# Half of the top-k searches moved from VectorE to ScalarE, and the distance bias from TensorE to VectorE

## The reference

```python
dots = jax.nn.relu(jnp.einsum('bqhd,bsd->bqhs', qib, k_idx).astype(jnp.float32))
score = jnp.einsum('bqh,bqhs->bqs', wb.astype(jnp.float32), dots)
score = jnp.where(visible[None], score, -jnp.inf)
_, idx = lax.top_k(score, topk)
...
logits = jnp.einsum('bqhd,bqkd->bhqk', qb, kg).astype(jnp.float32) * (HEAD_DIM ** -0.5)
logits = logits - slopes[None, :, None, None] * dist[:, None]
probs = jax.nn.softmax(logits, axis=-1).astype(v.dtype)
```

## Time and profile before

| | us |
|---|---|
| median of 3 runs (lowest to highest) | 3513.35 (3512.68 to 3517.88) |
| the profiled execution | 3499.91 |
| its span | 3498.0 |
| PE, DVE, ACT, POOL busy | 3099.7, 2084.9, 1290.0, 123.4 |

### The profile page before, as it was taken

One profiled execution on the slowest core, in us unless ns is written; L12 is line 12 of the kernel. 1 busy time (PEld: TensorE's weight loads), 2 busy tenths in 40 slices (PEclk: granted clock), 3 DMA queues, 4 the chain that ended last, 5 costly groups with the idle time before them and its releaser, 6 DMA issues. The chain is left out here.

```text
span 3498.0 us, 44638 instructions
## 1 busy us (share of the span) xinstructions
PE 3099.7 (89%) x15457; PEld 2525.6 (72%) x15457; DVE 2084.9 (60%) x4217; ACT 1290.0 (37%) x2575; POOL 123.4 (4%) x245
## 2 busy tenths in 40 slices
PE   6798888888888887876889699999999999999997
PEld 3576676677666666665778588788878888788876
DVE  2168888889999998989545444324442444244422
ACT  1364445444454444453443222222222322232222
POOL 0000000000000000000001100000000000000000
PEclk8788889887888888797999899999999999999999
DMA  5011100000000000000046533334333433343333
GB/s 202 21 46 31 37 25 25 19 25 25 22 10 19 22 19 10 10 4 7 4 160 180 165 93 96 90 120 144 96 96 114 138 97 97 112 144 96 96 92 107
DMA packets 316083, 254.97 MB, mean 73 GB/s; under 512 B 9153, under 2 KB 271905, under 8 KB 315809
## 3 DMA queue, kind: packets, MB, share of 16 engines
q1 hardware_dynamic: 282544, 236.29, 21.9%
q10 hardware_dynamic: 33392, 16.81, 1.7%
HBM read 219.50 MB, written 33.57 MB: 72 GB/s over the span
## 5 line engine op out<-in xcount | busy, mean ns | idle before, releaser
L1125 DVE TENSOR_SCALAR_CACHE_REDUCE above<-score,cand 128x384 bf16<-128x384 f32 (+13 forms) x448 | 661.9, 1478 | 9.0
L1865 DVE TENSOR_TENSOR p_lo<-raw,p_hi 128x1024 fp32r<-128x1024 f32 x264 | 323.4, 1225 | 422.6 <-ACT p_hi L1791 422.4
L1791 ACT ACTIVATE p_hi<-raw 128x1024 fp32r<-128x1024 f32 x264 | 279.3, 1058 | 690.9 <-PE dbank L1762 351.9
L984 ACT ACTIVATE probT<-tbank 128x512 f32<-128x512 f32 (+3 forms) x448 | 217.5, 488 | 506.3 <-PE tbank L713 503.8
L1175 DVE TENSOR_SCALAR_CACHE_REDUCE logit<-lbank 128x512 f32<-128x512 f32 (+3 forms) x448 | 246.7, 553 | 199.5 <-PE lbank L698 197.2
L729 PE MATMUL obank<-vb,probT 128*128 128x64 f32 x2176 | 303.4, 283 | 8.0 <-ACT probT L984 7.1
L591 PE MATMUL work<-w_in,h_T 128*128 128x512 f32 (+1 forms) x768 | 303.5, 545 | 0.7 <-ACT h_T L793 0.7
L729 PEld LDWEIGHTS obank<-vb,probT 128*128 128x128 f32 x2176 | 293.0, 206 | 13.9 <-ACT probT L984 13.4
L1743 PE MATMUL gbank<-x_hi,p_hi 128*128 128x512 f32 x704 | 275.1, 391 | 29.1 <-DVE p_lo L1865 29.1
L1760 PE MATMUL dbank<-p_hi,a_hi 128*128 128x512 f32 x704 | 277.1, 394 | 17.0 <-DVE a_lo L1893 14.1
L1761 PE MATMUL dbank<-p_lo,a_hi 128*128 128x512 f32 x704 | 276.2, 392 | 0.0
(11 more groups left out here) (202 smaller groups left out, 5231.7 us busy)
## 6 DMA issues: line engine op xcount, KB each, us to landing
raw<-in_w_gate_up SPq DMA_DIRECT2D x176, 512.0 KB, 3.8
raw<-in_w_down SPq DMA_DIRECT2D x88, 512.0 KB, 3.7
ada<-in_w_ada ACTq DMA_DIRECT2D x32, 512.0 KB, 3.9
wada<-in_w_ada SPq DMA_DIRECT2D x4, 2048.0 KB, 15.5
x_in<-in_x SPq DMA_DIRECT2D x16, 512.0 KB, 3.8
mixT<-oT SPq DMA_DIRECT2D x32, 256.0 KB, 2.4
mix<-mixT SPq DMA_DIRECT2D x16, 512.0 KB, 6.5
x_rows<-in_x SPq DMA_DIRECT2D x16, 512.0 KB, 4.6
```

Of the source, the lines that this page charges most:

```text
L1125: link(nc.vector.tensor_scalar(above[:, 0:L], score[:, 0:L], cand[:].bitcast(F32), None, ALU.is_ge, ALU.add, accum_out=count[:]), between, 1)
L1791: nc.scalar.activation(p_hi[:, s], raw[:, s], ACT.Copy).then_inc(panel_high, 1)
L1865: nc.vector.tensor_tensor(p_lo[:, s], raw[:, s], p_hi[:, s].bitcast(F32), ALU.subtract).then_inc(panel_ready, 1)
```

## The change

Six things change.

1. Blocks with an odd number (3, 5, ... 15) are searched by ACT. One ACTIVATE with the function Sign over the L scores (L1108 of the new program, `sum_signs`) gives by its accumulator the number of scores below less the number above. POOL moves the candidate `pick` with three small instructions (`move_pick`), of which two stand behind the sum. After 32 bits DVE makes one last count (`count_next`, "above") and the ties.
2. The search of a block is spread over two iterations, b-2 and b-1, in proportion to weights (`slot_weight`: 3.0 for an A head, 2.5 + 0.45 (b+1) for a B head). So in each iteration one even block is searched by DVE and one odd block by ACT. `score` gets two buffers. A heads, projections and norms run one block further ahead (block b+2 in iteration b).
3. The third product of a piece is gone. DVE adds the bias as it reads the piece: one `tensor_tensor_reduce` in place of the copy, with the minimum of the negated logits as its sum, chained from piece to piece, so that the reduction over pieces is gone too. Where the slope was applied on PE, `w_uq` and the first columns of `w_in` are now divided by the slopes at the start.
4. The exponential is written in place, over `logit`, which has three buffers now; `prob` is gone.
5. The wait for `bias_ready` stands on DVE, no longer on PE.
6. POOL fills 31 powers of two at the start; the modulation's last steps move a little.

```diff
+def search_slots(b):
+    slots = []
+    for it in (b - 2, b - 1):
+        if it + 2 < NB:
+            slots += [(it, "A", h) for h in range(HEADS)]
+        slots += [(it, "B", h) for h in range(HEADS)]
+    vector, scalar = {}, {}
+    if searched_by_scalar(b):
+        wts = [slot_weight(kind, it) for it, kind, h in slots[:-2]]
+        for slot, r in zip(slots, spread(wts, len(ON_SCALAR))):
+            scalar[slot] = [(b, ON_SCALAR[n]) for n in r]
+        vector[slots[-2]] = [(b, AFTER_SCALAR[0])]
+        vector[slots[-1]] = [(b, action) for action in AFTER_SCALAR[1:]]
...
+                    link(nc.gpsimd.tensor_tensor(pick_next[:], pick[:], toward_int[:, max(k - 1, 0):max(k - 1, 0) + 1],
+                                                 ALU.add))
+                    pool.wait_ge(signs_summed, 32 * nth + j + 1)
+                    link(nc.gpsimd.tensor_scalar(pick_back[:], less_more[:], float(L - 2 * TOPK), toward[:, k:k + 1],
+                                                 ALU.is_gt, ALU.mult))
+                    nc.gpsimd.tensor_tensor(pick[:], pick_next[:], pick_back[:], ALU.subtract).then_inc(pick_ready, 1)
...
-                    nc.tensor.matmul(out, q_lo[kind][:, h, :], keys, start=False, stop=False)
-                    mm = nc.tensor.matmul(out, slope_id[:, h, :], bias_of(kind, b, o, n)[:, at:at + width],
-                                          start=False, stop=True)
+                    mm = nc.tensor.matmul(out, q_lo[kind][:, h, :], keys, start=False, stop=True)
...
+            def sum_signs(b, action):
+                act.wait_ge(relu_used, relus[0])
+                act.wait_ge(pick_ready, 34 * nth + j + 1)
+                nc.scalar.activation(signs[:, 0:L], score[:, b % 2, 0:L], ACT.Sign, scale=-1.0,
+                                     bias=pick[:].bitcast(F32), accum_out=less_more[:]).then_inc(signs_summed, 1)
...
-                nc.vector.tensor_scalar(logit[:, i % 2, o:o + n], lbank[m % 2][:, 0:n], 1.0, None,
-                                        ALU.mult, ALU.max, accum_out=(mx_sink[:, h, 0:1] if kind == "A" else mx[:, i % 2, c:c + 1])
-                                        ).then_inc(piece_read, 1)
+                least = mx[:, i % 2, c - 1:c] if c else neg_sink[:, h:h + 1] if kind == "A" else -LOWEST
+                into = negmax[:, i % 4:i % 4 + 1] if c == pieces - 1 else mx[:, i % 2, c:c + 1]
+                nc.vector.tensor_tensor_reduce(logit[:, i % 3, o:o + n], lbank[m % 2][:, 0:n], bias_of(kind, b, o, n),
+                                               scale=-SLOPES[h], scalar=least, op0=ALU.add, op1=ALU.min,
+                                               accum_out=into).then_inc(piece_read, 1)
```

More of the change, by code:

```diff
@@ L180, with searched_by_scalar, slot_weight, spread @@
 SEARCH = [("bit", j) for j in range(32)] + [("ties", 0), ("ties", 1)]
[L183 to L194, removed]
+ON_SCALAR = [("bit", j) for j in range(32)]
+AFTER_SCALAR = [("above", 0), ("ties", 0), ("ties", 1)]
+def searched_by_scalar(b):
+    return b % 2 == 1
+def slot_weight(kind, b):
+    return 3.0 if kind == "A" else 2.5 + 0.45 * (b + 1)
+def spread(weights, n):
+    whole, at, out = sum(weights), 0.0, []
+    for wt in weights:
+        first = round(n * at / whole)
+        at += wt
+        out.append(range(first, round(n * at / whole)))
+    return out
+def search_slots(b):
[11 more added lines that the diff above has]
+        vector[slots[-1]] = [(b, action) for action in AFTER_SCALAR[1:]]
+    else:
+        wts = [0.0 if (it, kind, h) == (b - 2, "B", HEADS - 1) else slot_weight(kind, it) for it, kind, h in slots[:-1]]
+        for slot, r in zip(slots, spread(wts, len(SEARCH) - 1)):
+            vector[slot] = [(b, SEARCH[n]) for n in r]
+        vector[slots[-1]] = [(b, SEARCH[-1])]
+    return vector, scalar
 MOD_STEPS = 4 * D // P
@@ L226, in front_a, with modulate @@
               5: [("proj", b, 3)], 6: [("proj", b, 4)]}.get(h, []))
[L228 to L231, removed]
-    for b in range(NB):
[L233 to L239, removed]
+    def modulate():
+        nonlocal mods
+        if mods < MOD_STEPS:
+            add(("mod", mods))
+            mods += 1
@@ L240, in mixing_steps @@
+    for b in range(2):
+        for h in range(HEADS):
+            steps.append(("head", "A", b, h, (), ()))
+            front_a(b + 1, h)
+            if b and h in (1, 7):
+                modulate()
+        steps += [("queries", "A", b + 1), ("gains", b + 1), ("latent", b + 1), ("latent_up", b + 1),
+                  ("norm", b + 2)]
+    for b in range(NB):
+        nxt = b + 2 if b + 2 < NB else None
+        if nxt:
+            steps.append(("scores", nxt))
+        else:
             steps.append(("queries", "B", b))
@@ L251, in mixing_steps @@
         for h in range(HEADS):
[L252 to L258, removed]
+            at = (b, "B", h)
+            steps.append(("head", "B", b, h, tuple(vector.get(at, ())), tuple(scalar.get(at, ()))))
@@ L531, in _ @@
                 if s[0] == "mod_rows":
+                    fill_affine()
+                    continue
+                if s[0] == "scores" and searched_by_scalar(s[1]):
+                    start_pick(s[1])
+                if s[0] == "head":
+                    for b, action in s[5] + tuple(x for x in s[4] if x[1][0] == "above"):
+                        move_pick(b, action)
+                if s[0:4] == ("head", "B", NB - 1, 0):
                     modulate()
-                    continue
                 if s[0] not in ("norm", "gains"):
@@ L1179, in maximum @@
[L1179 to L1184 removed]
+                if c == 0 and i >= 3:
+                    dve.wait_ge(pt_full, plan.group0[i - 2])
```

246 lines of the change are left out of this document (160 added, 86 removed).

## The result

| | before | after |
|---|---|---|
| median of 4 runs each, in turns, us | 3513.01 (3509.27 to 3517.88) | 3547.27 (3543.42 to 3552.1) |
| profiled execution (span) | 3499.91 (3498.0) | 3546.74 (3545.0) |
| last piece ends at | 1756.4 | 1797.7 |

The account below looks back on a forecast made before the run. PE was taken to bound A heads and DVE B heads. Terms -49 (A), -1 (B), -13 (blocks 14 and 15) and +4 (start) made -59 from 3499.9: 3441, plus 13.4 for the median, 3455 us; range 3420 to 3490, chance 0.40.

Parts of the forecast that it names:

- The step that failed: B heads: a phase lasts 8% longer than its busiest engine (4 to 12% seen), giving 32.4, 48.7 and 73.9 us.
- 1 us less for them and block 13's: All B phases together: -13 us from the search's move and +12 from the ties' wait, so -1.
- A heads: A phases, bound by PE: third products gone, search bits fewer, last phase 28 for 48.0 us; together -49 us.
- My bound of 2: A heads: the third product's 16 pieces per eight heads cost about 2 us a phase at the granted clock.
- Blocks 13 to 15: End of the kernel: iteration 13's B heads 7 us less, blocks 14 and 15 139 for 152.3 us, -13.
- Start: Before the first projection: scaling multiplications added, those on the unit matrix gone; 0 to 5.5 us, taken +4.
- The ties' wait: Last head but one of B phases: even blocks' ties wait for ACT, 2 us in iterations 1, 3, ... 11: +12.
- Sums of signs stall the pipeline: Rival, chance 0.17: B heads with alternating one and two sums cost the longer engine each; 54 us in iteration 8, 3525.
- The slow new piece: Rival, chance 0.10: DVE's new bias-adding piece runs at the scan's pace, 119 us more of DVE, +90: 3545.
- Free overlap: Rival, chance 0.20: A and B heads mix, idle time beside A heads serving B heads; 156 us at most, half gives 3375.
- POOL held up by DVE: Rival, chance 0.08: POOL's candidate steps behind a DVE scan wait up to 4.4 us, ACT behind them; +39, 3494.
- A bit's 1.94 us: B heads: price of one search bit on DVE for 1280 scores: count, accumulator read and two small steps.

Follow-up runs that it names:

- the second run: Changed kernel with the ties of even blocks put back in the last head, behind the norm they wait for: 3542.24 us, 1.0093.
- short signs: ScalarE sums signs of the first 128 columns only: changed kernel 3423.05 us, 0.9753; changed kernel with 9.0, 30.0, the ties last and the roots first 3344.34 us, 0.9531.
- the mended split: Changed kernel with A heads counting 9.0 instead of 3.0, ties last: 3469.69 us; with the roots first 3440.77; with 30.0 for VectorE's steps too 3434.13.
- the vector-only kernel: Changed kernel with every block searched by VectorE in one iteration, none by ScalarE, the new weights kept: 3592.31 us, 1.0234.
- 9.0: Changed kernel with the spreading's weight of an A head 9.0 instead of 3.0, ties of even blocks in the last head: 3469.69 us, 0.9877.
- the experiment with the third matmul: Changed kernel with each piece's first product made twice, so TensorE has the bias matmuls' work back: 3605.18 us, 1.0276.
- The vector-only kernel with the old split: Changed kernel, all search on VectorE in one iteration, old table for blocks 2 to 14 (21 or 18 of 34 steps beside A heads): 3510.76 us, 0.9998.
- 30.0: Changed kernel with A heads weighing 30.0 for VectorE's steps and 9.0 for ScalarE's, ties last, roots first: 3434.13 us, 0.9786.
- the ties last: Edit of the changed kernel: ties of even blocks go back to the last head, behind the norm they wait for; alone 3542.24 us, 1.0093.
- the roots first: Edit of the changed kernel: POOL does the gains' two roots before the pick steps of head B h0; alone 3543.2 us, with 9.0 and ties last 3440.77.
- the kernel before with a late split: Kernel before with its table alone changed, 10 search steps beside A heads and 24 beside B heads instead of 21 or 18 and 13 or 16: 3631.15 us, 1.0345.

## Why the prediction was wrong

**The step that failed** is "A phase is longer than its busiest engine ... I take 8%". The busy times it was applied to were good: iteration 3, ACT 30.0 forecast and 28.7 measured; iteration 8, DVE 45.1 and 42.7, ACT 41.8 and 41.3. The factor was 1.21, 1.40 and, in iteration 12, 1.42, instead of 1.04 to 1.12. For iterations 3 and 8 that gave 34.8 and 59.8 us for my 32.4 and 48.7; the B heads of blocks 0 to 12 grew by 97 us, where I had 1 us less for them and block 13's (some 20 of the 97 stood in the score phases before, as the second run shows). I had read the factor off stretches with one engine at 89 to 96%, so that it stood for the small gaps of an engine that nearly always has work. In the levelled stretch PE, which both others feed, waits for each of them in turn. These are its waits in the B heads of iteration 8, before (841.9 to 895.4 us) and after (925.9 to 985.7):

```profile
PE lbank L696 <- DVE logit L1175: 8.8, 4, 3.7
PE obank L729 <- ACT probT L984: 0.5, 1, 0.5
...
PE lbank L795 <- DVE mx L1315: 8.7, 4, 5.2
PE obank L826 <- ACT probT L1084: 8.4, 2, 4.8
```

Busy and waiting, PE makes up the stretch in both: 43.9 + 9.3 of 53.5 us, 42.5 + 17.1 of 59.8. With three engines at 41 to 43 of 60 us, each in order, and DVE and ACT with search steps between their own, nothing is hidden whole. The short signs put a number on it: 0.57 and 0.43 us of time for each microsecond of ACT's, with no engine over 71% busy in iteration 8 and 78% on the mended split.

**The sentence above it carried the cause, and I drew nothing from it.** I wrote that the new weights put most of the remaining search beside the B heads, as a reason for a small gain. It is the reason for the loss: a split of that kind costs 82 us in the vector-only kernel and 119 in the kernel before. With 9.0 the same ScalarE search is 76 us faster by the ratios than with 3.0.

**A heads: right in sign, undersized.** Forecast -49, measured -68; the experiment with the third matmul puts 41 us of the A phases on these matmuls, 2.9 a phase where I took 2, and the vector-only kernel with the old split, which lacks the matmuls and keeps the search, is 41 shorter there too. My bound of 2 came from spacings at the granted clock of two single pairs. The last A phase was forecast at 28 and took 27.0.

**Blocks 13 to 15.** Forecast -20 (7 and 13), measured +17: 250.8 us with PE at 200.9 and ACT at 155.3, the same failed factor, for my head costs were of one engine each. The vector-only kernel with the old split shows a price of running one block ahead: 34 us more than before, where the whole search of block 15 stands beside B heads. In the kernel after, 5 of its 32 sums have A heads beside them.

**Start.** Forecast +4, measured +12.5. The scaling is the first part: DVE's sixteen multiplications over `w_uq` and `w_in` take 4.5 us where the eight on the unit matrix took 1.1, and PE's first piece is 3.7 us later. The rest is between PE's first piece and the first score phase (before, the first B head), 97.8 for 89.1 us. I had not priced that the last part of block 2's front end stands alone there. In PE's timeline it runs from 179.0 to 194.4 us with no head beside it, and PE waits in it for DVE, 5.0 us for `lat` and 4.0 for `qi_lo`; before, the same steps stood between the B heads of block 0. No run moved it back.

**The ties' wait.** Forecast +12 with 0 and 30 as ends. The view shows 56.6 us of it, and undoing it 1.4 us by the ratios, whose intervals reach 6 us either way: near the lower end. What I missed was the gains' wait on POOL, 49.1 us in the view, worth nothing measurable there and 23 us on the mended split.

**The rivals.** Sums of signs stall the pipeline: its condition (over 53 us in iteration 8) was met at 59.8, and its side was right; its 3525 is 22 us short. The length of the sums does stretch these heads (short signs), but its mechanism, heads made uneven by one or two sums, isn't shown: no run evened them out, and a sum laid ahead of the exponential changed nothing that can be told. The slow new piece, whose 3545 was nearest of all, was near by luck: 691 and 751 ns for 512, where it needed 1.1 us. Its own sum was off as well, since the earlier trace rows give 0.42 us a piece above the copy (4.42 / 4 - 0.688) and not 0.53, so +94 and not +119 of DVE. Free overlap is out: idle time beside A heads stayed idle. POOL held up by DVE happened, and can have done little: ACT waited 47.5 us for picks in all, in 50 places, of up to 3.7 us, and of POOL's time only 16 us are such hold-ups. The views of POOL's last two lines of a bit (count, ns min/median/max) show the medians and how far single ones lie above them:

```profile
L601 POOL TENSOR_SCALAR pick_back<-less_more,toward x217: 290/295/2819, 261.4 to 1707.1; 128x1 int32<-128x1 f32 x109
...
L603 POOL TENSOR_TENSOR pick<-pick_next,pick_back x217: 189/189/2082, 261.8 to 1707.5; 128x1 int32<-128x1 int32 x109
```

Of these 434 steps 32 take over 1.3 times their median. Each of the 32 lies over a DVE instruction with two inputs in SBUF (a sum of scores, a split into high and low parts, a gain, the scan or another step of the ties) and ends 0.05 to 0.17 us behind it; the longest, 2.82 us, ends behind the scan. The 69 steps that lie over a new piece, with one input in PSUM, and over none of these, take their usual time, at most 1.10 times the median. The kernel before shows such hold-ups too. Thirteen of its weighted sums (L1104, 0.75 us at the median) start 0.3 to 0.4 us behind one of POOL's additions to `x_in` (L555, 2.47 to 2.54 us); they take 2.60 to 2.73 us and end 0.42 to 0.55 behind it. And POOL's L544, 192 ns at the median, takes up to 752 where it ends 0.05 us behind L1145 of the ties, which has one input of full width, in SBUF: two such inputs aren't what all of them share. A bit's 1.94 us in the prediction holds the two small steps that go to POOL, a sum of signs' 1.55 doesn't. Like for like, a count is 1.63 us on DVE (1.544 + 0.083) and a sum of signs 1.55 on ACT, measured (1.357 + 0.192).

**The vector-only kernel with the old split** closes the account of what the rest of the change does without the move: start +12, A phases -41, B heads +3 and +34, score phases -3, in all +5 us, and 0.9998 times the time of before.

## What to carry to other kernels

Where a side task is laid beside two kinds of stretch, price a step in each kind before anything else, from how idle the engines that carry it are there; moving work to another engine helps only as far as it doesn't leave the stretch that has room. A busiest-engine estimate with a small factor held here while one engine was at 90%. When a change levels three in-order engines (here at 70%), expect a good part of each further microsecond as time: it was 0.57 and 0.43 of it here. The length of a wait in the profile doesn't say what it is worth: the same edit of a queue gave 2 us, which is within the noise, and on another kernel 23.

The best version here is the changed kernel with 9.0 for ScalarE's steps, 30.0 for VectorE's, the ties last and the roots first: 3434.13 us, 0.9786 (0.9767 to 0.9805) of the time before, and 0.9782 with a sum ahead of the exponential.

## What the runs showed of the hardware that I had not expected

The granted clock was lower in many stretches where PE starved. In the B heads of iteration 5 PE was busy for 33.2 of 56.4 us at 0.68, and over the whole stretch the clock was 0.81 for 0.85 before, and PE's busy time fell by 32 us only (3099.7 to 3068.2 in all) where the third matmuls, put back, made 94 us of it (3161.9). Every record of the granted clock in the traces before and after is 0.50 or 1.00. In those B heads of iteration 5 it is 0.50 from 618.8 to 631.8 us and 1.00 from 632.4 to 638.6; behind the second product of a piece of 512 (L796) the next matmul starts 0.43 us later in the first window (from 623.46, and from 629.75 us) and 0.23 in the second (from 633.94). Part of the time that is left in the levelled stretches is thus paid at 0.50; how much of the 34 us that is, no run shows. The share of busy time alone doesn't order the stretches, though: the B heads of iteration 8 have 0.91 with PE busy for 38.8 of 54.2 us in the vector-only kernel with the old split, and 0.77 with 48.9 of 58.5 in the kernel before with a late split. The fused piece of 512 costs 60 ns more with a per-partition starting value (751, as the line with `mx` shows) than with a constant (691, the line without); at 384 columns it is 617 for 558 ns.
